# A bidirectional recurrence with each cell cut into a front and a back, the next front placed ahead of the back

## The reference, cut to what matters

```python
def step(carry, blk):                       # one chunk, all four heads
    C, n, m = carry
    ...
    w_intra = jnp.exp(D - m_t[..., None])
    s = jnp.einsum('bhtd,bhsd->bhts', qb, kb) * w_intra
    num = jnp.einsum('bhts,bhsv->bhtv', s, vb) + w_inter[..., None] * jnp.einsum('bhtd,bhdv->bhtv', qb, C)
    den = s.sum(-1) + w_inter * jnp.einsum('bhtd,bhd->bht', qb, n)
    h = num / jnp.maximum(jnp.abs(den), jnp.exp(-m_t))[..., None]
    ...
    C_new = decay[..., None, None] * C + jnp.einsum('bhs,bhsd,bhsv->bhdv', wk, kb, vb)
    n_new = decay[..., None] * n + jnp.einsum('bhs,bhsd->bhd', wk, kb)
    return (C_new, n_new, m_new), h
h = h_fwd + h_bwd                           # then a layer norm by head, an output gate, and w_out
```

## Time and profile before

| what | value |
|---|---|
| median of 3 runs | 4858.48 us (4855.19 to 4858.59) |
| time of the profiled execution | 4856.34 us |
| span from its first to its last instruction | 4854.6 us |
| TensorE busy | 4579.0 us, 94% of the span |
| mean granted TensorE clock, share of full | 0.976 |
| the 16 cells, from the first product of the first to the last numerator read | 358.9 to 509.6 us |

### The profile page before, as it was taken

How to read it: one execution, slowest core, us unless ns; L and a number is a source line. 1 busy time by engine, 2 the same in 40 slices (tenths; PEclk the granted TensorE clock), 3 DMA queues, 4 the chain that set the end, 5 groups by cost and what they waited for, 6 DMA issues and landing times.

```text
span 4854.6 us, 39345 instructions
## 1 busy us (share of the span) xinstructions
PE 4579.0 (94%) x15828; PEld 2478.2 (51%) x15828; DVE 1688.6 (35%) x2611; ACT 911.7 (19%) x1623; POOL 681.8 (14%) x582
## 2 busy tenths in 40 slices
PE   5999899999999999999999997799999899999999
PEld 3457444444444456554444445544799644444444
DVE  4234363333324123232995313434333322222100
ACT  2113230000002122221332113332333200000000
POOL 3001015323200000000552000000111003222000
PEclk9999999999999999999999998899999999999999
DMA  4410001111110100001101100010000111111201
GB/s 172 152 43 1 18 26 43 44 44 44 43 43 29 38 24 11 9 9 35 44 35 44 69 35 26 17 46 26 13 1 1 53 69 52 43 44 44 79 36 58
DMA packets 50481, 202.26 MB, mean 42 GB/s; under 512 B 5632, under 2 KB 7168, under 8 KB 49168
## 3 DMA queue, kind: packets, MB, share of 16 engines
q1 hardware_dynamic: 46656, 168.58, 9.6%
q0 software_dynamic: 3664, 31.41, 1.7%
HBM read 185.29 MB, written 14.68 MB: 41 GB/s over the span
## 4 chain that ended last, share of the span: by engine, by line
PE 91%; DVE 4%; ACT 2%; issue 2%; POOL 1%; DMA 0%; POOLq 0%; ACTq 0%; DVEq 0%; SPq 0%; PEldq 0%
PE bank L183 34%; PE bank L463 24%; PE bank L2099 8%; PE bank L2254 6%; PE bank L1412 2%; PE bank L1439 1%; PE bank L1443 1%; PE bank L2052 1%; PE bank L2035 1%; PE bank L1461 1%; PE bank L2044 1%; PE bank L297 1%; PE bank L1418 1%; PE bank L2232 1%; PE bank L1453 1%
## 5 line engine op out<-in xcount | busy, mean ns | idle before, releaser
L183 PE MATMUL bank<-H,ring 128*128 128x512 f32 x2624 | 1141.2, 596 | 31.2 <-DMA ring<-in_proj 21.0
L183 PEld LDWEIGHTS bank<-H,ring 128*128 128x128 f32 x2624 | 501.1, 191 | 662.4 <-issue 623.0
L183 PE MATMUL bank<-ABC,ring 128*128 128x512 f32 x1328 | 579.0, 596 | 20.7 <-issue 14.9
L183 PEld LDWEIGHTS bank<-ABC,ring 128*128 128x128 f32 x1328 | 251.8, 191 | 337.3 <-issue 328.4
L2254 PE MATMUL bank<-ABC,ring 128*128 128x512 f32 x704 | 304.1, 595 | 2.6 <-PEq L2242 2.6
L463 PE MATMUL bank<-H,ring 128*128 128x512 f32 x576 | 253.1, 592 | 0.0
L1727 DVE SCALAR_TENSOR_TENSOR bank<-ABC,params,bank 128x1024 f32<-128x1024 f32 x184 | 237.3, 1290 | 8.0
L2254 PEld LDWEIGHTS bank<-ABC,ring 128*128 128x128 f32 x704 | 134.3, 191 | 172.4 <-issue 169.0
L463 PEld LDWEIGHTS bank<-H,ring 128*128 128x128 f32 x576 | 109.4, 190 | 137.8 <-issue 137.8
L2099 PE MATMUL bank<-ring 128*128 128x128 f32 x1152 | 144.9, 280 | 5.3 <-DVE ring L2577 4.2
L1357 POOL TENSOR_TENSOR ABC<-ABC 128x1024 f32<-128x1024 f32 x48 | 113.4, 2362 | 220.4 <-ACT ABC L1570 214.6
(11 more groups left out here) (484 smaller groups left out, 5990.6 us busy)
## 6 DMA issues: line engine op xcount, KB each, us to landing
ABC<-in_ada SPq DMA_DIRECT2D x48, 512.0 KB, 6.3
ring<-in_gu SPq DMA_DIRECT2D x44, 512.0 KB, 4.2
ring<-in_up SPq DMA_DIRECT2D x32, 512.0 KB, 4.0
ring<-in_down SPq DMA_DIRECT2D x32, 512.0 KB, 4.3
ring<-in_conv_in SPq DMA_DIRECT2D x24, 512.0 KB, 4.3
ring<-in_ffn SPq DMA_DIRECT2D x16, 704.0 KB, 4.8
ring<-in_proj SPq DMA_DIRECT2D x16, 512.0 KB, 6.8
ring<-in_mix SPq DMA_DIRECT2D x16, 512.0 KB, 4.4
```

The source lines that it names most:

```text
L183: mm = nc.tensor.matmul(bank[:, 2 * (m % 2) + h, :], ring[:, s % RING, k * P:(k + 1) * P], rhs(k)[:, h * HALF:(h + 1) * HALF], start=(k == ...
```

## The change

The 16 cells are numbered n = 0 to 15. Each is cut in two on TensorE, VectorE and ScalarE: the front holds all that does not depend on the state (mask and row terms, query weights, turned values, scores, turned keys, and what ScalarE and VectorE make of them), the back the numerators, the reciprocal, the quotient and the state. The lists are written in the order front 0, front 1, back 0, front 2, back 1, and so on to front 15, back 14, back 15. `values`, `queries`, `keys_tok` and `probs_t` become pairs, used in turn. The values are transposed straight from A, without `values_in`, and the keys are turned by two transposes of 128 columns straight from A, behind the scores; `keys_bd` stays for the scores. GpSimd waits for the scores of cell n - 2 and no longer for the state of a cell. The head sums and their statistics stand at other places in the lists.

```diff
-            cell_pool = steps("cell_gpsimd", "low0 high0 stage0 low1 high1 stage1", NT)
...
+            cell_pool = steps("cell_gpsimd", " ".join(f"low{n} high{n}" for n in range(CELLS)))
+            cell_pe = steps("cell_tensor", in_turn(("bcast", "values", "scores", "keys"), ("out", "state")))
+            cell_act = steps("cell_scalar", in_turn(("weights", "keys"), ("out",)))
+            cell_dve = steps("cell_vector", in_turn(("queries", "values", "probs"), ("neg", "guard", "den", "recip", "state")))
             ripe = [4, 3, 5, 2, 6, 1, 0, 7]
             gate_order = [1, 2, 3, 0, 4, 5, 6, 7]
             head_pool = steps("heads_gpsimd", " ".join(f"sum{c}" for c in ripe[:6]))
...
-            values_in = carve(1024, "p (d h s) -> p d h s", d=2, h=4)
             weights_t = carve(512)
-            probs_t = carve(512)
-            values = carve(516, "p (h v) -> p h v", h=4)
-            queries = carve(256, "p (q t) -> p q t", q=2)
-            keys_tok = carve(512, "p (h k) -> p h k", h=4)
+            probs_t = [norm_room[:, 512 * n:512 * n + 512] for n in range(2)]
+            values = [carve(516, "p (h v) -> p h v", h=4) for _ in range(2)]
+            queries = [carve(256, "p (q t) -> p q t", q=2) for _ in range(2)]
+            keys_tok = [carve(512, "p (h k) -> p h k", h=4) for _ in range(2)]
             cell = carve(1032, "p (d h v) -> p d h v", d=2, h=4)
...
             pool.memset(keys_bd, 0.0)
-            pool.memset(keys_tok, 0.0)
-            pool.memset(values, 1.0)
+            for n in range(2):
+                pool.memset(keys_tok[n], 0.0)
+                pool.memset(values[n], 1.0)
             pool.memset(cell, 0.0).then_inc(*cell_zero.did("zeroed"))
             pool.wait_ge(*cell_zero.all())
-            for i in range(NT):
-                for d in range(2):
-                    c = chunk_of(i, d)
-                    pool.wait_ge(*cell_pe.after(i, f"state{d}"))
-                    for e in range(2):
-                        nc.gpsimd.tensor_copy(keys_bd[64 * e:64 * e + 64, d, e::2, :],
-                                              A[64 * e:64 * e + 64, 2:4, bass.ds(c * P, P)]).then_inc(
-                                                  *cell_pool.did(("low", "high")[e] + str(d)))
-                        pool.wait_ge(*cell_pool.after(i, ("low", "high")[e] + str(d)))
-                    nc.gpsimd.tensor_copy(values_in[:, d, :, :],
-                                          A[:, 4:8, bass.ds(c * P, P)]).then_inc(*cell_pool.did(f"stage{d}"))
-                for c in ripe[2 * (i - 5):2 * (i - 5) + 2] if i >= 5 else []:
-                    pool.wait_ge(*cell_act.after(i, "out1"))
+            def head_sums_of(i):
+                for c in ripe[2 * (i - 5):2 * (i - 5) + 2]:
+                    pool.wait_ge(*cell_act.after(0, f"out{2 * i + 1}"))
                     nc.gpsimd.tensor_tensor(sums[:, 0, c, :], sums[:, 0, c, :], sums[:, 1, c, :], ALU.add).then_inc(*head_pool.did(f"sum{c}"))
+            for n in range(CELLS):
+                i, d, c, now = cell_of(n)
+                if n >= 2:
+                    pool.wait_ge(*cell_pe.after(0, f"scores{n - 2}"))
+                for e, name in enumerate(("low", "high")):
+                    rows = slice(64 * e, 64 * e + 64)
+                    nc.gpsimd.tensor_copy(keys_bd[rows, d, e::2, :], A[rows, 2:4, now]).then_inc(*cell_pool.did(f"{name}{n}"))
+                    pool.wait_ge(*cell_pool.after(0, f"{name}{n}"))
+                if n in (13, 15):
+                    head_sums_of(n // 2 - 1)
+            head_sums_of(7)
...
@@ -856,53 +865,62 @@
             pe.wait_ge(*taken("dft"))
             pe.wait_ge(*rows_dve.all())
             pe.wait_ge(*cell_zero.all())
-            pe.sem_inc(*cell_pe.lead())
...
-                    pe.wait_ge(*before(cell_act, "keys"))
-                    pe.wait_ge(*before(cell_dve, "probs"))
...
-                    pe.wait_ge(*cell_pool.after(i, f"stage{d}"))
-                    for h in range(4):
-                        nc.tensor.transpose(bank[:, 2, h * P:(h + 1) * P], values_in[:, d, h, :], ident[:, :])
-                    pe.wait_ge(*cell_dve.after(i + 1, f"queries{d}"))
-                    for q in range(2):
-                        for e in range(2):
-                            mm = nc.tensor.matmul(bank[:, 1, 256 + q * P + 64 * e:256 + q * P + 64 * e + 64],
-                                                  keys_bd[:, d, 2 * q + e, :], ident[:, 64 * e:64 * e + 64],
-                                             start=True, stop=True)
-                    mm.then_inc(*cell_pe.did(f"turn{d}"))
-                    for h in range(4):
-                        mm = nc.tensor.matmul(bank[:, 3, h * P:(h + 1) * P], keys_bd[:, d, h, :], A[:, h // 2, now],
-                                              start=True, stop=True)
-                    mm.then_inc(*cell_pe.did(f"scores{d}"))
...
-                    pe.wait_ge(*cell_dve.after(i + 1, f"probs{d}"))
-                    pe.wait_ge(*before(cell_act, "out"))
...
-                    pe.wait_ge(*cell_act.after(i + 1, f"keys{d}"))
...
+            def cell_front(n):
+                i, d, c, now = cell_of(n)
+                if n:
+                    pe.wait_ge(*cell_act.after(0, f"weights{n - 1}"))
+                nc.tensor.matmul(bank[:, 0, :], ident[:, :], causal[:, d:d + 1, :].broadcast_to([P, 4, P]),
+                                 start=True, stop=False, skip_group_check=True)
+                for h in range(4):
+                    nc.tensor.matmul(bank[:, 0, h * P:(h + 1) * P], sel_head[:, 4 * d + h, :], r_r[:, now],
+                                     start=False, stop=True, skip_group_check=True)
+                if n:
+                    pe.wait_ge(*cell_act.after(0, f"keys{n - 1}"))
+                for q in range(2):
+                    mm = nc.tensor.matmul(bank[:, 1, q * P:(q + 1) * P], sel_pair[:, 2 * d + q, :], r_wi[:, now], start=True, stop=True)
+                mm.then_inc(*cell_pe.did(f"bcast{n}"))
+                if n:
+                    pe.wait_ge(*cell_dve.after(0, f"values{n - 1}"))
+                for h in range(4):
+                    mm = nc.tensor.transpose(bank[:, 2, h * P:(h + 1) * P], A[:, 4 + h, now], ident[:, :])
+                mm.then_inc(*cell_pe.did(f"values{n}"))
+                pe.wait_ge(*cell_pool.after(0, f"high{n}"))
+                if n:
+                    pe.wait_ge(*cell_dve.after(0, f"probs{n - 1}"))
+                for h in range(4):
+                    mm = nc.tensor.matmul(bank[:, 3, h * P:(h + 1) * P], keys_bd[:, d, h, :], A[:, h // 2, now], start=True, stop=True)
+                mm.then_inc(*cell_pe.did(f"scores{n}"))
+                pe.wait_ge(*cell_dve.after(0, f"queries{n}"))
+                for q in range(2):
+                    mm = nc.tensor.transpose(bank[:, 1, 256 + q * P:256 + (q + 1) * P], A[:, 2 + q, now], ident[:, :])
+                mm.then_inc(*cell_pe.did(f"keys{n}"))
+
+            def cell_back(n):
+                i, d, c, now = cell_of(n)
+                pe.wait_ge(*cell_dve.after(0, f"probs{n}"))
+                if n:
+                    pe.wait_ge(*cell_act.after(0, f"out{n - 1}"))
+                if n >= 2:
+                    pe.wait_ge(*cell_dve.after(0, f"state{n - 2}"))
+                for h in range(4):
+                    num = bank[:, 4 + h // 2, (h % 2) * 129:(h % 2) * 129 + 129]
+                    nc.tensor.matmul(num, probs_t[n % 2][:, h * P:(h + 1) * P], values[n % 2][:, h, :], start=True, stop=False)
+                    mm = nc.tensor.matmul(num, queries[n % 2][:, h // 2, :], cell[:, d, h, :], start=False, stop=True)
+                mm.then_inc(*cell_pe.did(f"out{n}"))
+                pe.wait_ge(*cell_act.after(0, f"keys{n}"))
+                if n:
+                    pe.wait_ge(*cell_dve.after(0, f"state{n - 1}"))
+                for h in range(4):
+                    mm = nc.tensor.matmul(bank[:, 6 + h // 2, (h % 2) * 129:(h % 2) * 129 + 129],
+                                          keys_tok[n % 2][:, h, :], values[n % 2][:, h, :], start=True, stop=True)
+                mm.then_inc(*cell_pe.did(f"state{n}"))
+            for n in range(-1, CELLS):
+                if n + 1 < CELLS:
+                    cell_front(n + 1)
+                if n >= 0:
+                    cell_back(n)
...
+            for n in range(-1, CELLS):
+                if n + 1 < CELLS:
+                    i, d, c, now = cell_of(n + 1)
+                    col = lambda k, h: token_cols[:, k, c, 32 * d + h:32 * d + h + 1]
+                    act.wait_ge(*cell_pe.after(0, f"bcast{n + 1}"))
+                    if n >= 0:
+                        act.wait_ge(*cell_dve.after(0, f"probs{n}"))
                     for h in range(4):
...
-                    last.then_inc(*cell_act.did(f"weights{d}"))
-                    act.wait_ge(*cell_pe.after(i + 1, f"turn{d}"))
-                    apart(act)
```

(82 more changed lines are left out.)

62 lines of the change are left out of this document (8 added, 54 removed).

## The result

| what | before | after |
|---|---|---|
| median, first measurement (4 runs each) | 4857.98 us | 4818.37 us (4817.24 to 4820.16) |
| ratio, 95% interval | | 0.9920 (0.9903 to 0.9937) |
| span of the profiled execution | 4854.6 us | 4816.5 us |
| zeroing starts to first mask | 3.19 us | 3.86 us |
| first mask to the first step of the head norms | 154.43 us | 119.55 us |

The gain was 39.6 us here, and 35.9 and 36.4 us when the same kernel was measured again beside the kernel before. Between executions both kernels scatter by some us (before 4848.9 to 4858.6 in all), so 36 us is the better figure. The forecast was a gain of 31.9 us.

The account below looks back on a forecast made before the run. The prediction took the stage as a chain through TensorE: cells of 6.69 instead of 8.69 us, plus clock, statistics, tail and zeroing, make 122.5 against 154.4 us, a gain of 31.9 from 4858.5, so 4826.6 us; range 4819 to 4840.

Parts of the forecast that it names:

- the sum: First product to head norms: 103.6 us plus clock, statistics, tail and zeroing gives 122.5, against 154.4 before; gain 31.9 us.
- the low end of the range: Whole kernel: 4819 us, for a clock that rises at once and groups following without small holes.
- Sum of a cell: TensorE's steps in one cell at full clock: 6.69 us instead of 8.69, front 3.99 and back 2.70.
- Further waits: TensorE's list: 11 waits a cell instead of 7; cost between 0 and 3.8 us, taken as 0.
- Slack of the others: VectorE and ScalarE in a cell: every wait in TensorE's list has over 2 us in hand.
- Zeroing: Before the first mask: two more GpSimd memsets put off TensorE's first product by 0.95 us.
- The clock at the start: First cells: TensorE's low clock costs an excess of 4.6 to 8.5 us, taken as 6.5.
- The bounds: Around 4826.6 us: 4822 to 4834, from clock 1.9 less or 2.0 more, waits up to 3.8, scatter 3.
- Statistics: Cell 14: the first pair's statistics delay the queries, so the turned keys wait 0.8 us, once.
- Tail: From numerators 14 ready to the head norms: 10.65 us, with GpSimd's last sums waiting for quotient 15.
- From there on nothing changes: From the first step of the head norms on: time unchanged, TensorE resuming at 0.50 of its clock.

Follow-up runs that it names:

- warm start: Changed kernel plus two thrown-away mask products on TensorE while GpSimd zeroes the buffers; 4816.00 us, ratio 0.9923 to the kernel before.
- all the small ones: Changed kernel plus head sums two cells earlier, two thrown-away mask products before the stage, 120 and 20 thrown-away transposes behind it; 4814.05 us, ratio 0.9917.
- only the direct turns: Kernel before, order and buffers kept, but values and keys turned by transposes straight from A; 4839.02 us, ratio 0.9968.
- the earlier head sums: Changed kernel with each pair of head sums on GpSimd waiting for the quotient of two cells earlier; 4819.66 us, ratio 0.9926.

## Why the prediction was right, and where it was off

The direction, the mechanism and the place were right: TensorE sets the pitch, the other engines follow, and the gain is that of the stage. The stage, counted from the zeroing, lost 157.62 - 123.41 = 34.2 us against the 31.9 of the sum. The median of the first measurement, 4818.4, lies 8.2 us below the forecast of 4826.6 and 0.6 us below the low end of the range: 2.3 of the 8.2 come from the stage, and the rest of that measurement's gain, 39.6 - 34.2 = 5.4 us, lies outside it. By the gain of 36 us that the later measurements give, the time would have been 4822.5, well inside. Term by term:

- Sum of a cell: 6.69 forecast, 6.77 measured. The transposed values took 0.50, not 0.43, and the scores 0.89, not 0.86. Over 16 cells 1.3 us too little.
- Further waits: 0 was right. In the cell above no hole is left, and TensorE is busy 87.80 of 87.80 us.
- Slack of the others: "every wait has over 2 us in hand" was wrong for one. The quotient has 2.8 us, but the queries only 0.86 us before the keys, and that is the wait that closed behind the statistics. The pitch did not move when VectorE got 2.2 us more work a cell.
- Zeroing: 0.95 forecast, 0.67 measured. The two memsets cost 0.93, as said, but the first mask follows the end of the last memset by 0.15 us instead of 0.41: TensorE no longer waits for an opening step of VectorE in between (L1147 in the earlier trace rows).
- The clock at the start: this is the mis-sized term. An excess of 6.5 us, between 4.6 and 8.5, was forecast from the place of the first long run of products of 128 rows. It was 7.3 / 2 = 3.65 us, 2.85 less, and below the low bound. The place was read off one execution: the kernel before was profiled once, and there the clock rose after 14.4 us. It rose after 7.3 to 9.5 us in every other kernel without a warm start, also in those with the old order or the old keys. With one and the same list of TensorE up to there, the third mask came 14.5 to 14.6 us behind the first in four profiles and 15.4 in three, and as work at 0.50 takes twice as long here, the low stretch differs by up to 2 us by itself. Whether the 14.4 us belong to the kernel before or to that execution is not known.
- The bounds: the range's low end, 4819, was said to allow for a clock that rises at once and for no holes between the groups, but these two take 6.5 + 5.4 us off 4826.6, to 4814.7; the forecast's upper bound adds up to 4835.4, not 4834. The low end was thus set 4 us above its own reasons. The holes stayed (0.95, 1.00, 0.53).
- Statistics: 0.8 forecast, 7.22 - 6.77 = 0.45 measured, the wait at the keys of cell 14 as foreseen.
- Tail: 10.65 forecast, about 10.5 measured; GpSimd's sums are in the chain, and 1.6 us of it go when they wait for less.
- Together 2.85 + 0.35 + 0.15 + 0.28 - 1.3 = 2.3, the difference.
- "From there on nothing changes": the time from the first step of the head norms to the end was 4341.3 us in the profile before and 4338.6 to 4338.7 in the three of the changed kernel. 1.7 us of this are the clock of the first `mix` records. In the other profiles without added transposes behind the stage, which run the same instructions there, it was 4334.8 to 4344.6 us: a scatter, which no edit here explains.

What the prediction did not say is that its parts are not separate. In the new order the direct turns are worth 0.68 us a cell (7.45 to 6.77), in the old order 0.72 (8.69 to 7.97), but behind scores that come first nothing (7.60 and 7.60). And of the 1.92 us of a cell, 1.09 can be had by exchanging two neighbours in TensorE's list. The split with its buffers, on top of that, gives 0.15 (7.60 to 7.45), and with the direct turns for the keys 0.83.

Left open are two things: why the low stretch differs between kernels that begin alike, and what makes the 4335 to 4345 us behind the stage differ between profiles.

## What to carry to other kernels

When an engine waits for another's short step, look first for work already in its list that does not depend on the answer, and put it behind the step that produces the input: here the keys covered the multiplication at no cost. Shortening such covering work gives nothing until other work takes its place, which is what splitting the cell into a front and a back does. Do not read the length of a low stretch at a stage's start off one execution: here it differed by up to 2 us with the same list.

## What was not expected of the hardware

- Two thrown-away products of 128x512 before the stage took TensorE from 0.50 to 1.00 before the first mask that counts (warm start) or at it (all the small ones), where the changed kernel ran 7.3 us at 0.50.
- 120 f32 transposes kept the granted clock at 1.00; a wait of 2.1 us behind the head turns was followed by 0.50. In the changed kernel a wait of 1.85 us at the same place was followed by 1.00.
- Copies of 128x512 from PSUM that follow each other at once on VectorE cost 0.55 us more each by busy time, a single one 0.69.
- The level rose 14.4 us after the first mask in the profile before, 8.1 us in the kernel with only the direct turns, 7.3 us in the changed one, and over 9.0 us with the earlier head sums, whose list is the same up to there.
